# Moving the low parts of the attention output from VectorE to GpSimd, and reordering the first eight output-projection chunks

## The chip, the cores and the metric

One NeuronCore of a Trainium2 chip runs the whole program. The metric is the device time of one execution in microseconds (us). The engines are called PE (TensorE; its weight loads are shown as PEld), DVE (VectorE), ACT (ScalarE), POOL (GpSimd) and SP (SyncE, which only issues DMAs here).

## The reference, cut to what matters

The program computes two transformer-like blocks on 256 tokens of width 2048. The part around the change is the end of the first block's mixer, a gated delta rule with 32 value heads of 128 columns, and the output projection behind it:

```
def gated_deltanet(h, w_in, conv_w, a_log, dt_bias, norm_w, w_out):
    proj = h @ w_in
    ...
    o = gated_delta_rule(q, k, v, g, beta)            # [1, 256, 32, 128]
    o = o * lax.rsqrt(jnp.mean(o * o, -1, keepdims=True) + NORM_EPS)
    o = (o.astype(h.dtype) * norm_w) * jax.nn.silu(z.reshape(B, S, GDN_V_HEADS, HEAD_DIM))
    return o.reshape(B, S, GDN_DV) @ w_out            # [256, 4096] @ [4096, 2048]
x = layer_norm(ALPHA_DN * x + (1 + ga1) * y, ln_g[i, 0], ln_b[i, 0])
```

`ga1` is one sixth of `silu(c) @ mod_w + mod_b`, of which the kernel computes the last two thirds (`ga1` among them) beside the delta rule.

## The kernel before, in words

Every fp32 matrix product is made of three products of rounded operands: each operand is split into a high part (a copy to fp32r) and a low part (operand minus high part). For the weights ACT writes the high part `wh` (L1391, L1582) and another engine the low part `wl`: POOL at L597 while the delta rule runs, DVE at L2069 afterwards. One chunk of weights is 128x1024 numbers (two k-tiles by 512 columns, 512 KB), loaded by SP into a ring of four raw buffers; the split copies stand in a ring of three (`RING`) until the mixer is done, then of four. A chunk costs PE twelve matmuls.

The mixer works in 8 iterations (`NIT`) of four value heads. In each, PE interleaves the steps of `delta(it)` (some 20 small dependent pieces, which pass results between PE, DVE and ACT) with the 24 chunks of the next projection, by `beside`: one chunk, one step, except behind the chunks 3, 4 and 23 (`PAUSE`). In the last iteration there is no next input projection, and `ochunk(c)`, c = 0 to 23, does 24 chunks of the output projection instead (L830): chunks 0 to 11 for the output columns 0 to 511 (bank `pg[0]`), 12 to 23 for 512 to 1023 (`pg[1]`), each over heads 0 to 23. What is left, the last 8 heads of these two column groups (8 chunks, t = 0 to 7), and then all 32 heads of the other two groups (t = 8 to 39), is done by the loop `for t in range(CK_FF)` through `tchunk` (L1117). `out_chunk(t)` gives the bank, the pair of heads and whether it is the bank's last chunk.

The stationary operand of these chunks is the mixer's output `oT`, which is split too: `o_high(i)` on ACT (L1598) and `o_low(i)` on DVE (L2060) do four heads each, i = 0 to 7, as 128x1024 instructions. The group i = 7 is the output of the last iteration. In the last iteration DVE runs the steps of `delta`, an `o_low` behind each of the first five, and `mods` (L1818, L1820), which multiplies and sums the modulation weights that POOL loads (L591); the buffers of these loads are two, so POOL issues a load only when DVE is done with the one two before.

Around the end of the last iteration DVE does, in this order: `oz = ob * zt` (L2003), `low(0,0,0)`, the sum `md1`, `low(0,0,1)`, `oz * rstd` (L2014, counted as `on`), then `finish`, which copies PE's transposes of `oz` to `oT` with the norm weight (L2027), `low(0,0,2)` and `o_low(7)`. PE does the transposes (L726) behind chunk t = 0, and behind t = 2 it spreads `ga1` over the partitions (`row_of`, L1133, 32 matmuls). ACT copies `ga1` to SBUF (`ga1_out`, L1613) behind its copy for chunk 6, and DVE's `beside(t)` multiplies a finished bank by `ga1`, adds the residual and takes statistics (L2109, L2254, L2113), in order in its own queue between two `low`s: for `pg[0]` at t = 5, for `pg[1]` at t = 7.

Of the kernel before, what the change touches and what calls it, by code (L numbers as in the profile page):

```python
# [26 lines left out]
NIT = NQK // 2  # L27
# [56 lines left out]
def out_chunk(t):  # L84

    if t < 8:
        return t // 2 % 2, 12 + 2 * (t // 4) + t % 2, t in (5, 7)
    return 2 + (t - 8) // 16, (t - 8) % 16, (t - 8) % 16 == 15
# [28 lines left out]
def build(nc, A, out):  # L117
    ctx = ExitStack()
    with ctx:
# [276 lines left out]
        s_oh = sem("s_oh")  # L396
        s_os = sem("s_os")
        s_hm = sem("s_hm")
        s_ht = sem("s_ht")
# [67 lines left out]
        def _(sp):  # L467
# [77 lines left out]

            for half in range(2):
                for g in range(2):
                    loads(0, 0, 4 * half + 2 * g, w_out[:, 24 + 4 * half:28 + 4 * half, :], 512 * g, 2)
            for g in range(2):
# [34 lines left out]
        def _(pool):  # L584
# [40 lines left out]

            def batch(it, last=False):
                restart()
                rows = gcT[0:2 * NH, 0:P].unsqueeze(1).broadcast_to([2 * NH, VH, P])
                pick = pick2[:, bass.ds(it * VH, VH)].unsqueeze(2).broadcast_to([2 * NH, VH, P])
                nc.gpsimd.tensor_tensor(rowm[0:2 * NH], rows, pick, ALU.mult).then_inc(s_g, 1)  # L630
                for t in range(2):
                    mod_load(it * 8 + 32, t)
                for t in range(1, 22):
                    low(it + 1, t + 2)
                    if t >= 6 and t % 2 == 0 and t <= 16:
                        mod_load(it * 8 + 32, t // 2 - 1)
                if not last:
                    for t in range(RING):
                        low(it + 2, t)

            gcT = gx[:, 3, :]
# [7 lines left out]
            with pool.Fori(0, NIT - 1) as j:  # L649
                batch(j)  # L650
            batch(NIT - 1, True)

# [70 lines left out]
        def _(pe):  # L723
# [93 lines left out]
            def ochunk(c):  # L817

                if c == 0:
                    pe.wait_ge(s_zo, NIT)  # L820
                if c == 12:
                    pe.wait_ge(s_cd, NIT * 2)
                pe.wait_ge(s_low, NIT * NCH + (c + 5))
                g, kp = c // 12, c % 12
                if c < 12:
                    pe.wait_ge(s_os, kp // 2 + 1)
                for h in range(TT):
                    for k in range(2):
                        for i, (x, w) in enumerate(((0, wh), (0, wl), (1, wh))):
                            m = nc.tensor.matmul(halves(pg[g])[:, h, :], o_s[x][:, 2 * kp + k, h * P:(h + 1) * P],  # L830
                                                 w[c % RING][:, k, :], skip_group_check=True,
                                                 start=(kp == 0 and k == 0 and i == 0), stop=False)
                m.then_inc(s_pk, 1)
# [258 lines left out]
            for j in range(NIT - 1):  # L1092
                steps = beside(delta(j), steps, lambda c: gchunk(j + 1, c))
            steps = beside(delta(NIT - 1), steps, ochunk)

            def chunk(j, per, c, bank, act, k0, first, last):
# [48 lines left out]
            for t in range(CK_FF):  # L1145
                g, k, last = out_chunk(t)
                if t < 8:
                    pe.wait_ge(s_os, k // 2 + 1)
                elif t == 8:
                    pe.wait_ge(s_ev, 1)  # L1150
                elif t == 24:
                    pe.wait_ge(s_ev, 2)
                tchunk(0, 0, t, pg[g % 2], o_s, 2 * k, g >= 2 and k == 0, last)
                if t == 0:
                    next(steps)
                if t == 2:
                    pe.wait_ge(s_v, NIT * len(VO))
                    for i in range(2):
                        m = row_of(pd[i], 2 * KD + 8 * i)
                    m.then_inc(s_pp, 1)  # L1160
# [174 lines left out]
        def _(act):  # L1335
# [297 lines left out]
            def prep3():  # L1633
                act.wait_ge(s_pp, 5)
                for c in range(2):
                    a(BC[:, :, c, :], pd[c][:].rearrange("p (t s) -> p t s", s=P), ACT.Copy).then_inc(s_ap, 1)
            stream(0, 0, 0, CK_FF, {3: ga1_out, 15: prep0, 19: prep1, 24: prep2, 38: prep3})

# [135 lines left out]
        def _(dve):  # L1774
# [145 lines left out]
            def delta(it, mods):  # L1920
# [82 lines left out]
                done(v.tensor_tensor(oz, ob, zt, ALU.mult))  # L2003
                if not mods:
                    low(0, 0, 0)
                PEw("md1")
                mod_sum(it, 1)
                if mods:
                    squares(it + 1)
                else:  # L2010
                    low(0, 0, 1)
                dve.wait_ge(s_v, bv + VO["oz"])
# [41 lines left out]
            iteration(NIT - 2)  # L2054

            def o_low(i):

                dve.wait_ge(s_oh, i + 1)
                k = slice(4 * i, 4 * i + 4)
                v.tensor_tensor(fl(o_s[1][:, k, :]), fl(oT[:, k, :]), fl(o_s[0][:, k, :]).bitcast(F32),  # L2060
                                ALU.subtract).then_inc(s_os, 1)
            o_low(0)
            finish(NIT - 2)
            o_low(1)

# [19 lines left out]
            for t in range(18):  # L2085
                next(steps, None)
                if t < 5:
                    o_low(t + 2)
                mods(NIT * 8 + 24, t)
            finish(NIT - 1)  # L2090
            low(0, 0, 2)
            o_low(7)

# [392 lines left out]
```

## Time and profile before

| | |
|---|---|
| runs | 2819.94, 2822.1, 2823.57 us (median 2822.1) |
| profiled execution | 2822.1 us, span 2820.5 us, mean granted clock 0.987 |
| PE busy | 2710.6 us, 96% of the span |
| PEld, DVE, ACT, POOL busy | 83%, 69%, 43%, 28% |
| 868 to 970 us (last iteration), POOL busy | 60.20 us of 102.00 |
| 868 to 970 us, DVE busy | 79.32 us of 102.00 |

The span is the profile's own clock; 1.6 us of the execution lie around it. The rows below are from stretches of this span. The last iteration of the mixer fills it from about 865 to 967 us, and the eight chunks t = 0 to 7 from 964 to 991 us.

### The profile page before, as it was taken

The numbers are of one execution on the slowest core, as the hardware profiler recorded it, in microseconds if no ns is written. First come the engines' busy times: TensorE is split into PE (matmuls) and PEld (weight loads), VectorE is DVE, ScalarE is ACT, GpSimd is POOL, SyncE is SP. The second block draws the span as 40 slices with busy tenths as digits, with TensorE's granted clock in tenths as the row PEclk, the third lists the DMA queues.
The fourth block names the chain that finished last, engine by engine and source line by source line (L and its number), as shares of the span: only waits on it lengthen the run. The fifth ranks groups of instructions, "written<-read, shape, count | busy, mean of one in ns | idle before, by whom it ended". The sixth has DMA issues, their size and how long they took to land.

```text
span 2820.5 us, 48695 instructions
## 1 busy us (share of the span) xinstructions
PE 2710.6 (96%) x18902; PEld 2338.9 (83%) x18902; DVE 1949.8 (69%) x2291; ACT 1208.1 (43%) x1521; POOL 798.1 (28%) x548
## 2 busy tenths in 40 slices
PE   6999999999998999999999999969999999999998
PEld 4688988898897887888888888769999998888886
DVE  1377877787788677666666666676999899555554
ACT  2255455545545444333333333344333334543443
POOL 1056666676666510000000000001565562000000
PEclk8999999999999999999999999989999999999999
DMA  9866666666675666666666555535455554666664
GB/s 364 311 193 208 235 203 198 220 233 196 208 239 178 222 206 203 194 189 189 187 188 190 187 186 186 169 114 171 151 172 156 157 171 156 191 187 191 187 205 146
DMA packets 283912, 552.59 MB, mean 196 GB/s; under 512 B 16817, under 2 KB 54258, under 8 KB 282610
## 3 DMA queue, kind: packets, MB, share of 16 engines
q1 hardware_dynamic: 263632, 474.02, 53.4%
q0 software_dynamic: 19408, 76.06, 7.2%
q8 instruction: 122, 2.00, 0.3%
q10 hardware_dynamic: 722, 0.28, 0.0%
q14 instruction: 28, 0.23, 0.0%
HBM read 548.19 MB, written 2.10 MB: 195 GB/s over the span
## 4 chain that ended last, share of the span: by engine, by line
PE 82%; DVE 10%; ACT 4%; issue 2%; DMA 1%; DVEq 0%; POOL 0%; ACTq 0%; SPq 0%; POOLq 0%; PEld 0%
PE pg L1117 26%; PE pd L1117 17%; PE pg L811 13%; PE pg L1104 9%; PE pg L802 4%; PE pd L726 2%; DVE wl L2069 2%; PE pg L830 2%; DMA arena<-in_mod_w 1%; PE pd L991 1%; PE pd L973 1%; DVE arena L2348 1%; DVE arena L2350 1%; DVE arena L2343 1%; PE pd L739 1%
## 5 line engine op out<-in xcount | busy, mean ns | idle before, releaser
L2069 DVE TENSOR_TENSOR wl<-wr,wh 128x1024 fp32r<-128x1024 f32 x616 | 773.7, 1265 | 505.5 <-ACT wh L1582 502.2
L1582 ACT ACTIVATE wh<-wr 128x1024 fp32r<-128x1024 f32 x616 | 652.6, 1060 | 987.3 <-PE pg L1117 390.4
L597 POOL TENSOR_TENSOR wl<-wr,wh 128x1024 fp32r<-128x1024 f32 x195 | 479.3, 2459 | 404.1 <-ACT wh L1391 403.9
L1391 ACT ACTIVATE wh<-wr 128x1024 fp32r<-128x1024 f32 x216 | 227.7, 1057 | 346.5 <-PE pg L811 219.9
L1104 PE MATMUL pg<-hh,wh 128*128 128x256 f32 x1280 | 366.3, 286 | 3.8 <-ACT arena L1700 2.5
L1104 PE MATMUL pg<-hl,wh 128*128 128x256 f32 x1280 | 362.9, 284 | 0.0
L1104 PE MATMUL pg<-hh,wl 128*128 128x256 f32 x1280 | 362.7, 283 | 0.0
L1117 PE MATMUL pg<-wh,hh 128*128 128x512 f32 x832 | 327.2, 393 | 0.0
L1117 PE MATMUL pg<-wl,hh 128*128 128x512 f32 x832 | 326.3, 392 | 0.0
L1117 PE MATMUL pg<-wh,hl 128*128 128x512 f32 x832 | 325.4, 391 | 0.0
L811 PE MATMUL pg<-hh,wh 128*128 128x256 f32 x1024 | 300.8, 294 | 14.8 <-ACT arena L1439 12.0
L1820 DVE SCALAR_TENSOR_TENSOR arena<-arena,condt 128x512 f32<-128x512 f32 x240 | 281.6, 1174 | 24.1 <-DMA arena<-in_mod_w 18.6
L811 PE MATMUL pg<-hl,wh 128*128 128x256 f32 x1024 | 289.6, 283 | 0.0
L811 PE MATMUL pg<-hh,wl 128*128 128x256 f32 x1024 | 289.4, 283 | 0.0
L1104 PEld LDWEIGHTS pg<-hh,wh 128*128 128x128 f32 x1280 | 246.0, 192 | 16.0 <-issue 13.3
L715 POOL COPY arena<-arena 128x256 f32 x8 | 6.4, 797 | 875.5 <-ACT arena L1700 875.5
L1104 PEld LDWEIGHTS pg<-hh,wl 128*128 128x128 f32 x1280 | 246.1, 192 | 0.0
L1104 PEld LDWEIGHTS pg<-hl,wh 128*128 128x128 f32 x1280 | 246.0, 192 | 0.0
L811 PEld LDWEIGHTS pg<-hh,wh 128*128 128x128 f32 x1024 | 196.1, 191 | 33.4 <-ACT arena L1439 14.6
L811 PEld LDWEIGHTS pg<-hl,wh 128*128 128x128 f32 x1024 | 196.2, 192 | 0.2 <-issue 0.2
L811 PEld LDWEIGHTS pg<-hh,wl 128*128 128x128 f32 x1024 | 196.1, 191 | 0.0
L1117 PEld LDWEIGHTS pg<-wh,hh 128*128 128x128 f32 x832 | 156.4, 188 | 34.9 <-issue 0.4
(390 smaller groups left out, 5016.5 us busy)
## 6 DMA issues: line engine op xcount, KB each, us to landing
wr<-in_w_in SPq DMA_DIRECT2D x224, 512.0 KB, 3.9
wr<-in_ffn_w_gu SPq DMA_DIRECT2D x176, 512.0 KB, 4.2
wr<-in_gdn_w_in SPq DMA_DIRECT2D x128, 512.0 KB, 4.0
arena<-in_mod_w POOLq DMA_DIRECT2D x64, 1024.0 KB, 6.8
wr<-in_ffn_w_down SPq DMA_DIRECT2D x88, 512.0 KB, 3.8
arena<-in_mod_w SPq DMA_DIRECT2D x32, 1024.0 KB, 12.0
wr<-in_gdn_w_in SPq DMA_DIRECT2D x128, 256.0 KB, 2.9
wr<-in_gdn_w_out SPq DMA_DIRECT2D x56, 512.0 KB, 4.6
```

Of the source, the lines that this page charges most:

```text
L597: nc.gpsimd.tensor_tensor(wl[c % RING][:], wraw[c % 4], wh[c % RING][:].bitcast(F32), ALU.subtract)\
L726: return nc.tensor.transpose(dst, src, ident[0:n, 0:n])
L739: m = nc.tensor.matmul(pd[0][32 * i:32 * i + 32, 0:512], condt[:, k + i:k + i + 1].broadcast_to([P, 32]), wm[t % 6][:, i, :], start=(k == ...
L802: m = nc.tensor.matmul(halves(bank)[:, t, :], h_s[x][:, 2 * kp + k, t * P:(t + 1) * P], w[c % RING][:, k, :], skip_group_check=True, start ...
L811: m = nc.tensor.matmul(bank[:, n * T:(n + 1) * T], w[c % RING][:, k, n * P:(n + 1) * P], h_s[x][:, 2 * kp + k, :], skip_group_check=True, ...
L830: m = nc.tensor.matmul(halves(pg[g])[:, h, :], o_s[x][:, 2 * kp + k, h * P:(h + 1) * P], w[c % RING][:, k, :], skip_group_check=True, star ...
L1104: m = nc.tensor.matmul(bank[:, n * T:(n + 1) * T], w[s][:, k, n * P:(n + 1) * P], act[x][:, k0 + k, :], skip_group_check=True, start=(firs ...
L1117: m = nc.tensor.matmul(halves(bank)[:, h, :], act[x][:, k0 + k, h * P:(h + 1) * P], w[s][:, k, :], skip_group_check=True, start=(first and ...
L1391: a(wh[c % RING][:], wraw[c % 4], ACT.Copy).then_inc(s_hi, 1)
L1582: a(wh[c % 4][:], wraw[c % 4], ACT.Copy).then_inc(s_hc, 1)
L1820: m = stt(out=dst, in0=mw[t % 2][:, k, :], scalar=condt[:, kk:kk + 1], in1=dst, op0=ALU.mult, op1=ALU.add)
L2069: v.tensor_tensor(wl[c % 4][:], wraw[c % 4], wh[c % 4][:].bitcast(F32), ALU.subtract).then_inc(s_lc, 1)
```

## The change

Six of the eight `o_low` instructions (i = 1 to 6) go from DVE to POOL; the groups 0 and 7 stay on DVE and get a semaphore of their own, `s_osv`. The chunks t = 0 to 7 no longer alternate between the banks: four for `pg[0]`, then four for `pg[1]`. PE transposes the last heads ahead of chunk t = 0, `ga1` is spread behind t = 4, ACT copies it behind its copy for chunk 8, and DVE finishes `pg[0]` at t = 3. DVE's `low(0,0,0)` and `low(0,0,1)` go behind the last `delta` step.

```
-        return t // 2 % 2, 12 + 2 * (t // 4) + t % 2, t in (5, 7)
+        return t // 4, 12 + t % 4, t % 4 == 3
...
-            for half in range(2):
-                for g in range(2):
-                    loads(0, 0, 4 * half + 2 * g, w_out[:, 24 + 4 * half:28 + 4 * half, :], 512 * g, 2)
+            for g in range(2):
+                loads(0, 0, 4 * g, w_out[:, 24:32, :], 512 * g, 4)
...  POOL, last iteration
+                if o_low:
+                    o_low(1)
                 for t in range(2):
                     mod_load(it * 8 + 32, t)
                 for t in range(1, 22):
+                    if o_low and t < 6:
+                        o_low(t + 1)
                     low(it + 1, t + 2)
...
+            def o_low(i):
+                pool.wait_ge(s_oh, i + 1)
+                k = slice(4 * i, 4 * i + 4)
+                nc.gpsimd.tensor_tensor(flat4(o_s[1][:, k, :]), flat4(oT[:, k, :]), flat4(o_s[0][:, k, :]).bitcast(F32),
+                                        ALU.subtract).then_inc(s_os, 1)
...  PE
-                if c < 12:
-                    pe.wait_ge(s_os, kp // 2 + 1)
+                if c == 0:
+                    pe.wait_ge(s_osv, 1)
+                elif 2 <= c < 12:
+                    pe.wait_ge(s_os, kp // 2)
...
             steps = beside(delta(NIT - 1), steps, ochunk)
+            next(steps)
...
                 if t < 8:
-                    pe.wait_ge(s_os, k // 2 + 1)
+                    pe.wait_ge(s_os, 6)
+                    if k >= 14:
+                        pe.wait_ge(s_osv, 2)
...
-                if t == 0:
-                    next(steps)
-                if t == 2:
+                if t == 4:
                     pe.wait_ge(s_v, NIT * len(VO))
...  ACT
-            stream(0, 0, 0, CK_FF, {3: ga1_out, 15: prep0, 19: prep1, 24: prep2, 38: prep3})
+            stream(0, 0, 0, CK_FF, {5: ga1_out, 15: prep0, 19: prep1, 24: prep2, 38: prep3})
...  DVE, last iteration
             for t in range(18):
                 next(steps, None)
-                if t < 5:
-                    o_low(t + 2)
                 mods(NIT * 8 + 24, t)
+            low(0, 0, 0)
+            low(0, 0, 1)
             finish(NIT - 1)
```

POOL at the start of the last iteration, before. `rowm` is L630; `mod_w` rows are the modulation loads; the three `wl` buffers are the low parts of the chunks 3, 4, 5, 6, 7, 8 in turn.

```order
L630 TENSOR_TENSOR arena<-arena,masks 64x512
L591 DMA arena<-in_mod_w 128x4x512 x2
L597 TENSOR_TENSOR wl0_61<-wr,wh0_57 128x1024
L597 TENSOR_TENSOR wl1_62<-wr,wh1_58 128x1024
L597 TENSOR_TENSOR wl2_63<-wr,wh2_59 128x1024
```

The same place now; `ol` is the low part of `oT`.

```order
L630 TENSOR_TENSOR arena<-arena,masks 64x512
L650 TENSOR_TENSOR ol_52<-arena,oh_51 128x1024
L591 DMA arena<-in_mod_w 128x4x512 x2
L650 TENSOR_TENSOR ol_52<-arena,oh_51 128x1024
L597 TENSOR_TENSOR wl0_61<-wr,wh0_57 128x1024
L650 TENSOR_TENSOR ol_52<-arena,oh_51 128x1024
L597 TENSOR_TENSOR wl1_62<-wr,wh1_58 128x1024
L650 TENSOR_TENSOR ol_52<-arena,oh_51 128x1024
L597 TENSOR_TENSOR wl2_63<-wr,wh2_59 128x1024
```

One `ol` stands ahead of the two loads, and one ahead of each of the low parts of the chunks 3 to 7.

DVE at the end of the last iteration, before.

```order
L2003 TENSOR_TENSOR arena<-arena 128x1024
L2069 TENSOR_TENSOR wl0_61<-wr,wh0_57 128x1024
L2019 TENSOR_REDUCE arena<-pd0 128x4
L2022 TENSOR_TENSOR modt<-arena,vc 128x4
L2069 TENSOR_TENSOR wl1_62<-wr,wh1_58 128x1024
L2014 TENSOR_TENSOR arena<-arena 128x1024
L2027 TENSOR_SCALAR arena<-pd1,vc 128x2x4x128
```

The same place now (L2018 is the former L2003, L2025 the former L2014, L2038 the former L2027).

```order
L2018 TENSOR_TENSOR arena<-arena 128x1024
L2030 TENSOR_REDUCE arena<-pd0 128x4
L2033 TENSOR_TENSOR modt<-arena,vc 128x4
L2025 TENSOR_TENSOR arena<-arena 128x1024
L2074 TENSOR_TENSOR wl0_61<-wr,wh0_57 128x1024
L2074 TENSOR_TENSOR wl1_62<-wr,wh1_58 128x1024
L2038 TENSOR_SCALAR arena<-pd1,vc 128x2x4x128
```

The product for the transposes stands two `wl` instructions earlier.

DVE at the chunks t = 2 to 4 now: the low parts of the chunks 5 and 6, the small factors, the finishing of bank `pg0`, and the low part of chunk 7 (`wl3`) and of chunk 8.

```order
L2074 TENSOR_TENSOR wl1_62<-wr,wh1_58 128x1024
L2074 TENSOR_TENSOR wl2_63<-wr,wh2_59 128x1024
L447 ISA
L2105 TENSOR_SCALAR arena<-modt 128x16
L2106 TENSOR_TENSOR arena<-vc,arena 128x16
L2107 TENSOR_TENSOR arena<-vc,arena 128x16
L2108 TENSOR_TENSOR arena<-arena,modt 128x16
L447 ISA
L2116 TENSOR_TENSOR pg0<-pg0,arena 128x1024
L2261 SCALAR_TENSOR_TENSOR arena<-arena,pg0 128x2x512
L2120 BN_STATS arena<-arena 128x6 x2
L2074 TENSOR_TENSOR wl3_64<-wr,wh3_60 128x1024
```

Before, the low parts of the chunks 7 and 8 stood ahead of the finishing of `pg0`.

## Rows read from the trace of the kernel before

**Rows 1.** PE's timeline: start us, us, engine, line, operation, operands, [idle before, releaser].
```profile
880.76 0.39 PE L830 MATMUL pg<-wh,oh 128*128 128x512 f32 x1
...
892.65 1.15 PE L973 MATMUL pd<-arena 64*64 64x64 f32 x32 [1.87 <-DVE arena L1963]
893.73 0.50 PE L830 MATMUL pg<-wh,oh 128*128 128x512 f32 x1
...
898.69 1.83 PE L991 MATMUL pd<-arena 64*64 64x64 f32 x32 [1.95 <-DVE arena L1971]
```

**Rows 2.** Chain that ended last, 855 to 1010 us: start us, us, piece.
```profile
886.22 2.79 DVE arena L1820
...
900.52 3.82 PE pg L830 x12
...
905.41 2.94 PE pg L830 x12
```

**Rows 3.** Busy time in windows: length, PE, PEld, DVE, ACT, POOL, PEclk, DMA, GB/s.
```profile
899.00:902.00 3.00, 3.00 (x34) 2.59 (x31) 3.00 (x2) 0.00 (x0) 1.33 (x1) 0.50 0.50 128
...
970.00:983.00 13.00, 13.00 (x75) 11.09 (x74) 6.00 (x6) 5.27 (x7) 8.35 (x14) 1.00 0.91 312
```

**Rows 4.** POOL's timeline, last iteration and the one before it.
```profile
766.93 1.03 POOL L630 TENSOR_TENSOR arena<-arena,masks 64x512 f32<-64x512 f32 x1
...
867.07 2.02 POOL L630 TENSOR_TENSOR arena<-arena,masks 64x512 f32<-64x512 f32 x1
869.04 1.56 POOL L591 DMA_DIRECT2D arena<-in_mod_w  x2
...
882.61 8.63 POOL L597 TENSOR_TENSOR wl<-wr,wh 128x1024 fp32r<-128x1024 f32 x3 [0.99 <-ACT wh L1391]
...
894.18 2.40 POOL L597 TENSOR_TENSOR wl<-wr,wh 128x1024 fp32r<-128x1024 f32 x1 [1.32 <-ACT wh L1391]
```

**Rows 5.** DVE's timeline, last iteration.
```profile
884.23 1.98 DVE L2060 TENSOR_TENSOR ol<-arena,oh 128x1024 fp32r<-128x1024 f32 x1
...
894.16 3.75 DVE L1820 SCALAR_TENSOR_TENSOR arena<-arena,condt 128x512 f32<-128x512 f32 x2
...
904.63 1.53 DVE L1820 SCALAR_TENSOR_TENSOR arena<-arena,condt 128x512 f32<-128x512 f32 x2
```

**Rows 6.** Chain that ended last, the chunks t = 0 to 7.
```profile
963.85 3.01 PE pg L1117 x12
966.86 1.06 PE pd L726 x8
...
973.51 3.57 PE pd L1133 x32
977.08 32.92 PE pg L1117 x143
```

**Rows 7.** ACT's timeline, end of the iteration and `ga1_out`.
```profile
963.42 0.21 ACT L1527 ACTIVATE arena<-arena 128x8 f32<-128x8 f32 x1
...
982.78 1.02 ACT L1614 ACTIVATE arena<-pd 128x1024 f32<-128x1024 f32 x1
...
985.22 1.06 ACT L1582 ACTIVATE wh<-wr 128x1024 fp32r<-128x1024 f32 x1 [0.48 <-DMA wr<-in_gdn_w_out]
```

**Rows 8.** DVE's timeline, end of the iteration and the finishing of `pg[0]`.
```profile
965.56 1.22 DVE L2014 TENSOR_TENSOR arena<-arena 128x1024 f32<-128x1024 f32 x1
967.96 1.28 DVE L2027 TENSOR_SCALAR arena<-pd,vc 128x1024 f32<-128x1024 f32 x1 [1.19 <-PE pd L726]
969.16 1.22 DVE L2069 TENSOR_TENSOR wl<-wr,wh 128x1024 fp32r<-128x1024 f32 x1
...
987.46 1.23 DVE L2109 TENSOR_TENSOR pg<-pg,arena 128x1024 f32<-128x1024 f32 x1
988.72 1.22 DVE L2254 SCALAR_TENSOR_TENSOR arena<-arena,pg 128x1024 f32<-128x1024 f32 x1
989.98 1.43 DVE L2113 BATCH_NORM_STATS2 arena<-arena 128x6 f32<-128x512 f32 x2
```

More of the change, by code:

```diff
@@ L397, in build @@
         s_os = sem("s_os")
+        s_osv = sem("s_osv")
         s_hm = sem("s_hm")
@@ L624, in _, with batch @@
                                         pattern=[[2 * s, nb], [0, s]], channel_multiplier=-1).then_inc(s_cst, 1)
-            def batch(it, last=False):
+            def batch(it, o_low=None):
                 restart()
@@ L636, in batch @@
                         mod_load(it * 8 + 32, t // 2 - 1)
-                if not last:
+                if not o_low:
                     for t in range(RING):
                         low(it + 2, t)
+            def o_low(i):
+                pool.wait_ge(s_oh, i + 1)
+                k = slice(4 * i, 4 * i + 4)
+                flat4 = lambda x: x.rearrange("p a b -> p (a b)")
+                nc.gpsimd.tensor_tensor(flat4(o_s[1][:, k, :]), flat4(oT[:, k, :]), flat4(o_s[0][:, k, :]).bitcast(F32),
+                                        ALU.subtract).then_inc(s_os, 1)
             gcT = gx[:, 3, :]
@@ L650, in _ @@
                 batch(j)
-            batch(NIT - 1, True)
+            batch(NIT - 1, o_low)
             restart()
@@ L2003, in delta @@
                 done(v.tensor_tensor(oz, ob, zt, ALU.mult))
-                if not mods:
-                    low(0, 0, 0)
                 PEw("md1")
@@ L2009, in delta @@
                     squares(it + 1)
-                else:
-                    low(0, 0, 1)
                 dve.wait_ge(s_v, bv + VO["oz"])
@@ L2054, in _ @@
             iteration(NIT - 2)
[L2056 to L2062, printed above, removed]
+            dve.wait_ge(s_oh, 1)
+            v.tensor_tensor(fl(o_s[1][:, 0:4, :]), fl(oT[:, 0:4, :]), fl(o_s[0][:, 0:4, :]).bitcast(F32),
+                            ALU.subtract).then_inc(s_osv, 1)
             finish(NIT - 2)
-            o_low(1)
             def low(j, per, c):
@@ L2086, in _ @@
                 next(steps, None)
-                if t < 5:
-                    o_low(t + 2)
                 mods(NIT * 8 + 24, t)
+            low(0, 0, 0)
+            low(0, 0, 1)
             finish(NIT - 1)
             low(0, 0, 2)
-            o_low(7)
+            dve.wait_ge(s_oh, 8)
+            v.tensor_tensor(fl(o_s[1][:, 28:32, :]), fl(oT[:, 28:32, :]), fl(o_s[0][:, 28:32, :]).bitcast(F32),
+                            ALU.subtract).then_inc(s_osv, 1)
             def factors():
```

## The prediction

> **What bounds the kernel now.** I read the page first: PE is busy in 96% of the span, so a wait of PE that is added or removed moves the end, and nearly nothing else does. Then the chain of waits and PE's own timeline in the last iteration of the mixer, to see where PE waits there. Between 868 and 899 us it does. It waits 1.87 us and 1.95 us for DVE [rows 1], and where it starts again the granted clock is 0.50, so at its lower level of 1.2 GHz [rows 3]: a group of twelve matmuls takes 3.82 us instead of 2.94 [rows 2]. Behind 905 us the chain stays on PE until 1010 us, with no wait longer than an issue gap. The reader should see two regimes in one iteration: up to 899 us the small engines set the pace, and from 905 us PE does.
>
> The third view is the pair of timelines of POOL and DVE in the same stretch. DVE's two instructions of L1820 take 1.53 us together when POOL is idle (the one at 904.63) [rows 5], that is 0.77 each. In the chain at 886 us each takes 2.8 us [rows 2]. POOL then does three instructions in a row, 8.63 us from 882.61, so 2.88 each instead of 2.40 [rows 4]. At 894.18 POOL starts one of 2.40 us and DVE's pair beside it takes 3.75 us [rows 4, 5]: it ends at 897.91, which is POOL's end at 896.58 plus 1.33. So a DVE instruction with two operands in SBUF doesn't run beside a POOL instruction; it waits for its end, and POOL in turn waits about 0.5 us for it. The page "SBUF — State Buffer" of the Trainium skill, section "Who interferes with whom", says that such a pair shares a port as an exclusive lock and that the order of issue decides who waits; by that rule too, the trace agrees.
>
> **Part one: six `o_low` go to POOL.** On DVE one of them is 1.2 us alone and up to 2.9 beside POOL (1.98 in [rows 5]). On POOL it has the shape of `low`, so 2.40 us alone and 2.88 where DVE's instructions come between. POOL's queue is in order, and the new order puts one ahead of the low part of each of the chunks 3 to 7, which PE needs. The step count:
> - `rowm` (1.03 us uncontended [rows 4]) starts at 867.1 as before [rows 4] and ends about 868.1. It took 2.02 there because an `o_low` of DVE stood in its way, now gone. `o_low(1)` ends at 870.5, the two loads (1.56 us [rows 4]) at 872.1, 1.5 us later than before. DVE's product behind `rn` now finds POOL issuing loads and loses no time; it keeps POOL off until 872.8.
> - Two instructions per chunk: low(3) at 877.4 (PE asks for it a chunk ahead of 880.76, at 878.0: no wait), low(4) at 882.3 (2 x 2.40 plus a short DVE piece). PE asked at 880.76 [rows 1]: 1.5 late.
> - From here DVE always has something that wants the port, so a pair is 2 x 2.88 = 5.76 us: low(5) at 888.1, low(6) at 893.8, low(7) at 899.4. PE asked for chunk 7 at 893.73 [rows 1], so that chunk is 5.7 late.
> - What is given back: PE's old wait of 1.95 behind chunk 7 disappears behind the new one, and so may the half clock, which cost 3.82 - 2.94 = 0.9 on the group and some 1.2 on the 32 small matmuls ahead of it (1.83 us [rows 1], against about 0.6 for such a piece at full clock). With chunk 7 ending at 902.2 and DVE's next answer about 1.1 later, chunk 8 runs from 903.9 to 906.9. Before it ended at 904.3 (900.52 + 3.82 [rows 2]). That is 2.5 late.
> - What is then taken again: DVE's own queue. It has lost the `o_low`, but five L1820 and other two-operand pieces that met an idle POOL now each meet a busy one and wait up to 2.4 us. I put the reply for chunk 9 at 909.3, so it runs from 910.4 where it ran from 905.41 [rows 2]: 5.0 late. From chunk 10 on PE sets the pace again, without slack in which to catch up.
>
> By this walk the iteration ends 4.5 us late (between 4 and 5; I take off a half because my handover at each port change is rounded up). Bounds: if POOL and DVE did not disturb each other at all, ten POOL instructions of 2.40 from 872.1 end at 896.1, chunk 7 is 2.4 late, and the old wait and half clock behind it (1.95 + 2.1) come back: -1.7. If every handover goes against PE and DVE, +7. That the mod loads are issued 1.5 us later costs nothing beyond this; DVE asks for them about as late.
>
> The page "Perfetto Trace Analysis" of the Trainium skill, section "Optimizing Scalar/DVE Operations", warns that moving work between GpSimd and DVE might not help since they share a read port. By that rule alone the relief of DVE would be about nothing; it leaves open who is in the queue behind, which is where I put the loss.
>
> **Part two: the end of the iteration and the eight chunks.** Let C be the end of PE's last mixer chunk, 963.8 before. Before, chunk t = 0 starts at C [rows 6], and PE does eight chunks of 2.76 us (32.92 / 143 x 12 [rows 6]), the transposes (1.06) and `row_of` (3.57), 26.7 us without a wait.
> - Now the transposes come first. They need DVE's L2014, which needs `rstd`, done by ACT at 963.63 [rows 7], so C - 0.2. DVE's 1.22 [rows 8] gives C + 1.1, the transposes C + 2.2. Chunk t = 0 needs `low(0,0,0)`, which follows L2014, at C + 2.2 as well. Eight chunks and `row_of` are 25.65, so without further waits C + 27.9: 1.1 us lost. `o_low(7)`, needed at t = 2 now (C + 7.7), is done at C + 6.9: `finish` 1.2, `low` 1.2 and itself 1.2 behind C + 3.4 [rows 8]. No wait.
> - Chunk 7's low part now stands behind the finishing of `pg[0]` in DVE's queue, which waits for `ga1`. `row_of` ends at C + 2.2 + 5 x 2.76 + 3.57 = C + 19.6; ACT's two copies of about 1.0 [rows 7] end at C + 21.5; DVE's 1.23 + 1.22 + 1.43 [rows 8] at C + 25.4; low(7) at C + 26.6. PE asks for it at C + 2.2 + 7 x 2.76 + 3.57 = C + 25.1. A wait of 1.5.
> - ACT's copy for chunk 8 stands ahead of `ga1_out`, and it needs its DMA. Before, one of these copies waited for its DMA until 985.22, C + 21.4 [rows 7], with 312 GB/s and a DMA share of 0.91 from 970 to 983 us [rows 3]: the residual `x` and four weight chunks land together. Now two more weight chunks are asked for just ahead of this burst, because their buffers come free later. If chunk 8's DMA lands at C + 21.4 again, `ga1` is ready at C + 24.4, low(7) at C + 29.5, and PE waits 4.4.
>
> So part two costs 1.1 + 1.5 = 2.6 at least and 1.1 + 4.4 = 5.5 where DMA is late. I take 4, the middle, as the burst is shifted by some 2 us and widened by 1 MB. What the edit gives, an earlier finished `pg[0]`, is worth nothing: chunk t = 8, which needs it, ran without a wait before (the 143 matmuls of [rows 6] have no gap). Swapping the order of the weight loads moves the same bytes: nothing, between -0.3 and +0.3 by the 0.48 us wait in [rows 7].
>
> **Sum.** 4.5 + 4.0 = 8.5 us on the profiled execution's own 2822.1 (span 2820.5 and 1.6 around it), which is also the median of the runs: 2830.6 us. All that follows is paced by PE or by loads that follow PE, so the delay is carried to the end.
>
> **Rivals.**
> 1. *POOL keeps up, and DVE's relief is what counts* (faster). The chain from 872 to 899 us runs through DVE, and if chunk 7's low part were ready before 893.7 the waits 1.87 + 1.95 and the half clock, 2.1, would go: -5.9, less 2.6 of part two: -3.3, so 2818.8. Against it: ten POOL instructions do not fit in 872.1 to 893.7 even at 2.40. It decides at that one time. 6%.
> 2. *Both small* (no difference that shows). Port conflicts cost little, -1.7, part two 2.6 to 4: +0.9 to +2.3; or one of the two parts is half of what I say, up to +5: 2823 to 2827. 19%.
> 3. *The clock falls more often* (slower still). By the walk above PE now waits some 1.5, 3.0, 1.4, 1.7 and 2.4 us between 880 and 910 us. Before, two waits of 1.9 were followed by a stretch at the lower level that cost 2.1. Two such stretches on chunks where PE sets the pace add 2 x 2.1: 2834.8. For it: DVE and POOL hide only what falls into their waits. 17%.
> 4. *The forecast*, 2827 to 2833. 58%.
>
> **Range and chances.** The forecast's own range is 2826.5 to 2833. Taking in the case without port conflict with a prompt DMA (2823) and the sum of both upper ends, 7 + 5.5 with one more clock stretch of 2.1 (2836.7), I give 2823 to 2836.5. Two tenths of a percent, 5.6 us, is about what this measurement can tell from no change. Rival 1 gives 5% faster; rival 2 and the low edge of the forecast 21% within; the rest 74% slower.
>
> **What would show it.** In the new profile POOL's instructions stand back to back from 872 to 902 us, and PE waits for POOL's L597 line (its new number) ahead of the chunks 4 to 7: about 1.5, 3, 1.4 and 1.7 us. The time per group of twelve matmuls behind 915 us is unchanged. The transposes come 1.1 us behind the last mixer chunk. PE waits for DVE's low part ahead of t = 7, between 1.5 and 4.4 us, and the releaser of DVE's finishing of `pg[0]` is ACT's copy of `ga1`. I am wrong if POOL has gaps ahead of chunk 7's low part, if DVE's L1820 take 0.8 us each beside a busy POOL, or if chunk 8's DMA has landed before `row_of` ends, which would take 2 to 3 us off.

## The result, and the profile after

| | before | changed |
|---|---|---|
| median of the runs | 2822.84 us (2819.94 to 2824.7) | 2840.74 us (2836.88 to 2842.76, 4 runs) |
| ratio | | 1.0064, 95% interval 1.0051 to 1.0078 |
| profiled execution, span | 2822.1, 2820.5 us | 2838.75, 2836.8 us |
| mean granted clock | 0.987 | 0.984 |

The changed kernel is slower by 17.9 us. The forecast was 2830.6 us, 8.5 slower, with a range that ended at 2836.5: the sign was right, the size was not. Here is the same chain of waits as in [rows 2], of the changed kernel (start us, us, piece):

```profile
870.89 9.26 DVE arena L1948
880.19 3.69 PE pd L936 x16
...
904.79 4.76 DVE arena L1835
909.57 0.76 DVE arena L1835
910.36 0.70 DVE arena L1991
911.10 1.12 PE pd L738 x4
```

One DVE instruction of 9.26 us stands in it: L1948, the product behind `rn` (q and k times their inverse norms), 128x1024 with both operands in SBUF. Before, it took 2.47 us; alone such a shape takes 1.2 (1.23 in `port_guard` below). POOL's timeline beside it, the answer to [rows 4]:

```profile
868.15 1.56 POOL L591 DMA_DIRECT2D arena<-in_mod_w  x2
869.73 2.36 POOL L650 TENSOR_TENSOR ol<-arena,oh 128x1024 fp32r<-128x1024 f32 x1
872.05 2.39 POOL L597 TENSOR_TENSOR wl<-wr,wh 128x1024 fp32r<-128x1024 f32 x1
874.41 2.34 POOL L650 TENSOR_TENSOR ol<-arena,oh 128x1024 fp32r<-128x1024 f32 x1
876.72 2.33 POOL L597 TENSOR_TENSOR wl<-wr,wh 128x1024 fp32r<-128x1024 f32 x1
884.32 2.42 POOL L650 TENSOR_TENSOR ol<-arena,oh 128x1024 fp32r<-128x1024 f32 x1 [5.27 <-ACT oh L1613]
886.70 2.87 POOL L597 TENSOR_TENSOR wl<-wr,wh 128x1024 fp32r<-128x1024 f32 x1
```

Four instructions stand back to back from 869.73 to 879.05, and DVE's, which begins at 870.89, ends at 880.15, 1.1 us after POOL ran dry. Three times POOL passed from one instruction to the next and DVE was not let in between. From 884 us on the two do alternate, as the prediction had it: POOL's take 2.8 us instead of 2.4. Not everywhere, though: DVE's first L1835 in the chain above, 4.76 us from 904.79, is held in the same way, past one handover of POOL, until these two are over:

```profile
904.26 4.72 POOL L597 TENSOR_TENSOR wl<-wr,wh 128x1024 fp32r<-128x1024 f32 x2
```

The kernel before (product, and POOL's row beside it):

```profile
871.60 2.47 DVE L1933 TENSOR_TENSOR arena<-arena 128x1024 f32<-128x1024 f32 x1 [3.32 <-ACT arena L1467]
```

```profile
870.61 2.36 POOL L597 TENSOR_TENSOR wl<-wr,wh 128x1024 fp32r<-128x1024 f32 x1
873.54 2.77 POOL L597 TENSOR_TENSOR wl<-wr,wh 128x1024 fp32r<-128x1024 f32 x1 [0.57 <-ACT wh L1391]
```

There POOL happened to wait 0.57 us for ACT at 872.97, and the product ended 1.1 us after POOL fell idle. PE's waits in the changed kernel, the answer to [rows 1]:

```profile
880.19 3.68 PE L936 MATMUL pd<-arena 128*128 128x128 f32 x16 [5.21 <-DVE arena L1948]
...
895.20 0.50 PE L844 MATMUL pg<-wh,oh 128*128 128x512 f32 x1 [0.80 <-POOL wl L597]
...
900.77 0.50 PE L844 MATMUL pg<-wh,oh 128*128 128x512 f32 x1 [1.44 <-POOL wl L597]
...
904.84 1.15 PE L1005 MATMUL pd<-arena 64*64 64x64 f32 x32 [1.06 <-DVE arena L1986]
...
911.10 1.12 PE L738 MATMUL pd<-ident,arena 128*128 128x128 f32 x4 [2.14 <-DVE arena L1991]
...
973.42 1.09 PE L738 MATMUL pd<-ident,arena 128*128 128x128 f32 x8 [1.22 <-DVE arena L2025]
...
1002.23 0.77 PE L1132 MATMUL pg<-wh,oh 128*128 128x512 f32 x1 [4.55 <-DVE wl L2074]
```

The last two belong to part two. The chain into the last one, the answer to [rows 6] and [rows 7]; the mixer's last chunk ends at 972.2, which is C now:

```profile
981.48 12.40 DMA wr<-in_gdn_w_out
993.90 1.06 ACT wh L1597
994.96 0.05 ACT arena L1628
...
995.77 1.02 ACT arena L1629
...
996.88 1.24 DVE pg L2116
998.14 1.23 DVE arena L2261
999.40 0.70 DVE arena L2120
1000.13 0.70 DVE arena L2120
1000.86 1.24 DVE wl L2074
```

ACT's copy for chunk 8 (993.90) waits for its DMA ahead of the copy of `ga1`, DVE's finishing of `pg[0]` waits for that, and chunk 7's low part (1000.86) stands behind it. Behind three of these waits the granted clock is at its lower level, as in [rows 3]: it falls at 880.3, 911.0 and 999.7 us, where the kernel before has one such stretch, at 899 us. Two of the three (window: length, PE, PEld, DVE, ACT, POOL, PEclk, DMA, GB/s):

```profile
880.00:884.00 4.00, 3.81 (x19) 3.81 (x20) 3.38 (x12) 1.76 (x2) 0.00 (x0) 0.57 0.44 131
...
999.00:1007.00 8.00, 4.77 (x12) 3.83 (x13) 6.39 (x7) 0.00 (x0) 0.00 (x0) 0.57 0.42 133
```

What these stretches cost can be read from how far PE's starts shift against the other kernel, which does the same matmuls at full clock: 1.7, 1.5 and 1.9 us, against 1.3 us for the one of before. PE's waits of 0.45 us and more (without one of 0.91 for ACT at 871 us that both kernels have) add up to 10.65 us in the mixer, against 3.82 before, and to 5.77 in the tail, against none.

For all kernels one reading serves best: the start of matmul number k less that of number k before. All have 18,902 matmuls, so this shows where time is lost. In the profiled executions (us; the columns are times of the kernel before; "mixer" and "tail" are the differences between columns):

| kernel | at 845 | at 963 | at 1050 | mixer | tail | median less before's |
|---|---|---|---|---|---|---|
| changed | -2.2 | 8.4 | 16.2 | 10.6 | 7.8 | +17.9 |
| low_moved_only | -2.6 | 9.9 | 9.7 | 12.5 | -0.1 | +7.8 |
| tail_only | -0.5 | 1.1 | 7.2 | 1.6 | 6.1 | +4.6 |
| port_guard | -2.7 | 4.6 | 9.3 | 7.3 | 4.7 | +10.4 |
| ga1_before_copy8 | -2.4 | 10.7 | 15.5 | 13.1 | 4.8 | +13.5 |
| tail_row_of_early | -2.5 | -2.5 | -1.4 | 0.0 | 1.1 | +2.0 |
| loads_behind | -0.9 | 7.8 | 7.7 | 8.7 | -0.1 | +8.4 |
| spread | -2.9 | 12.7 | 12.6 | 15.7 | -0.1 | +14.2 |
| spread_guard | -2.3 | 9.7 | 9.6 | 12.0 | -0.1 | +10.9 |
| tiny_gap | -2.4 | 8.6 | 15.2 | 11.0 | 6.6 | +15.1 |
| o_low_later_on_dve | -2.5 | -0.4 | -0.5 | 2.1 | -0.1 | +1.3 |
| guard_row_of_early | -0.2 | 7.1 | 8.2 | 7.2 | 1.1 | +7.8 |
| half_on_pool | -2.5 | 3.3 | 4.4 | 5.9 | 1.1 | +4.3 |

Three cautions. Before 845 us no kernel differs from the one before, and all are 0.2 to 2.9 us ahead: that is what one execution differs from another by, and since all are ahead, it is mostly the profiled execution of before that is late. In the changed kernel's mixer 1.5 of the 10.6 us fall on a stretch at the lower clock level at 860 us, before anything the change touches delays PE; the change's part is 9.1. With the same POOL and DVE edits in the mixer, `low_moved_only` and `ga1_before_copy8` lose 12.5 and 13.1 there, so one execution gives part one only to some 4 us. And the differences of the medians, each against the runs of before on the same chip at the same time, are uncertain by 2.5 to 4 us by their intervals.

### The profile page after: what moved, and what is told of

Its sections match the earlier page's. It is cut to its first block, busy times and chain, and to the rows that moved or that the text cites. A ratio compares the mean times of both kernels' runs of the same rounds, so it can differ in the third digit from the quotient of the medians.

```text
span 2836.8 us, 48694 instructions
## 1 busy us (share of the span) xinstructions
PE 2715.5 (96%) x18902; PEld 2341.8 (83%) x18902; DVE 1948.6 (69%) x2285; ACT 1208.2 (43%) x1521; POOL 812.2 (29%) x554
## 4 chain that ended last, share of the span: by engine, by line
PE 80%; DVE 11%; ACT 4%; issue 2%; DMA 2%; DVEq 0%; POOL 0%; ACTq 0%; SPq 0%; POOLq 0%; PEld 0%
PE pg L1132 25%; PE pd L1132 17%; PE pg L823 13%; PE pg L1119 9%; PE pg L814 4%; DVE wl L2074 2%; PE pd L738 2%; PE pg L844 2%; DMA arena<-in_mod_w 1%; PE pd L987 1%; PE pd L1005 1%; DVE arena L2355 1%; DVE arena L2357 1%; DVE arena L2350 1%; ACT arena L1477 1%
## 5 line engine op out<-in xcount | busy, mean ns | idle before, releaser
L1597 ACT ACTIVATE wh<-wr 128x1024 fp32r<-128x1024 f32 x616 | 652.7, 1060 | 997.7 <-PE pg L1132 405.4
L1835 DVE SCALAR_TENSOR_TENSOR arena<-arena,condt 128x512 f32<-128x512 f32 x240 | 281.1, 1171 | 29.3 <-DMA arena<-in_mod_w 23.7
```

The costliest lines, as they stand in the source:

```text
L1597: a(wh[c % 4][:], wraw[c % 4], ACT.Copy).then_inc(s_hc, 1)
L1835: m = stt(out=dst, in0=mw[t % 2][:, k, :], scalar=condt[:, kk:kk + 1], in1=dst, op0=ALU.mult, op1=ALU.add)
```

## The experiments

The two parts apart. `low_moved_only` has the six `o_low` on POOL, with the chunks t = 0 to 7, the transposes, DVE's two `low`, `row_of` and `ga1_out` as before; `tail_only` is the rest of the diff, with the `o_low` on DVE.

> Part one alone: the six o_low on GpSimd, the eight chunks, the transposes, row_of, ga1_out and DVE's two low parts as before the change. Theory A (a DVE instruction with two SBUF operands is kept off the port by POOL instructions that follow each other without a gap, until POOL runs dry): DVE's product behind rn takes 8 to 10 us again instead of 1.2 or 2.5, PE waits about 5 us for it, and the kernel is 9 to 12 us slower than before. Rival B (only POOL's throughput, 2.4 to 2.9 us an instruction, as I forecast): 4 to 6 us slower, with the waits on POOL's low parts. Rival C (the two parts need each other): under 4 us.

> Part two alone: all o_low on DVE as before the change; new order of the eight chunks, transposes first, row_of behind t = 4, ga1_out behind the copy for chunk 8. If the parts add up: 1.1 us for the transposes and a wait of 1.5 to 4.5 us ahead of t = 7, and 2 to 3 us of half clock behind that wait, so 5 to 9 us slower than before. If the wait in the changed kernel came from part one's delay of the loads, it is under 2 us and the kernel is 1 to 3 us slower.

Measured: `low_moved_only` 2831.3 us (2830.48 to 2835.36), ratio 1.0036, interval 1.0022 to 1.0049; `tail_only` 2828.11, ratio 1.002, interval 1.0011 to 1.0029. Both parts cost. Neither median decides between its outcomes: 7.8 us slower lies below the 9 to 12 of theory A and above the 4 to 6 of rival B, and 4.6 below the 5 to 9 of parts that add up. The medians' 7.8 and 4.6 make 12.4, 5.5 less than the 17.9 of both together, which their intervals allow; in the traces the parts do add up, 12.5 and 6.1 against 10.6 and 7.8. So it is the trace that tells. Part one alone has the long product, longer still (10.77 us), and PE waits for it:

```profile
879.83 3.51 PE L937 MATMUL pd<-arena 128*128 128x128 f32 x16 [6.73 <-DVE arena L1950]
```

Here the product, by its start, is even first: POOL is still issuing its loads, and the row of instructions begins 0.38 us later. DVE, then POOL:

```profile
869.01 10.77 DVE L1950 TENSOR_TENSOR arena<-arena 128x1024 f32<-128x1024 f32 x1 [4.97 <-ACT arena L1484]
```

```profile
867.82 1.56 POOL L592 DMA_DIRECT2D arena<-in_mod_w  x2
869.39 2.39 POOL L651 TENSOR_TENSOR ol<-arena,oh 128x1024 fp32r<-128x1024 f32 x1
```

In `tiny_gap` and `spread` below it is the same, 0.37 and 0.41 us. Part two alone has the wait ahead of t = 7 behind the same chain, and a stretch at the lower clock level behind it (993.3 to 996.7 us):

```profile
993.79 0.77 PE L1118 MATMUL pg<-wh,oh 128*128 128x512 f32 x1 [3.46 <-DVE wl L2063]
```

Is it POOL's row that holds the product? `port_guard` is the changed kernel where POOL waits until the product is done before it starts `o_low(2)`. This adds a wait and takes no work away.

```
                 pool.wait_ge(s_oh, i + 1)
+                if i == 2:
+                    pool.wait_ge(s_v, (NIT - 1) * len(VO) + VO["qkn"])
```

> The changed kernel with one wait more: POOL waits for DVE's product behind rn before it does o_low(2). Theory A: DVE gets the port at once, the product takes 1.2 us instead of 9.3, PE's 5.2 us wait for it goes, what is left is POOL's throughput; 5 to 8 us faster than the changed kernel, so 10 to 13 us slower than before. Rival B (POOL's throughput alone): POOL starts its ten instructions about 0.7 us later and the kernel is 0 to 1 us slower than the changed one, 18 to 19 us slower than before.

Measured: 2833.92 us (2833.34 to 2835.55), ratio 1.0044, interval 1.003 to 1.0058, 6.8 below the changed kernel and as theory A had it. The product is back to the time that it takes alone, and POOL pays 1.0 for it; DVE's row and then POOL's:

```profile
868.94 1.23 DVE L1950 TENSOR_TENSOR arena<-arena 128x1024 f32<-128x1024 f32 x1 [4.96 <-ACT arena L1484]
```

```profile
870.32 2.41 POOL L652 TENSOR_TENSOR ol<-arena,oh 128x1024 fp32r<-128x1024 f32 x1 [1.01 <-DVE arena L1950]
```

So the cause of the product's 9 to 11 us is shown: POOL's row of instructions. Its price by the table is the mixer's 9.1 (product 9.3 us) or 12.5 (product 10.8) less 7.3, so 1.8 to 5.2 us; another 3.1 lie in the tail, 7.8 against 4.7, where the guarded execution had no stretch at the lower level and a wait of 3.5 instead of 4.5; that the guard is the cause of these is not shown. What then remains are the waits for POOL that the prediction had named:

```profile
880.43 0.50 PE L846 MATMUL pg<-wh,oh 128*128 128x512 f32 x1 [2.21 <-POOL wl L597]
...
885.54 0.50 PE L846 MATMUL pg<-wh,oh 128*128 128x512 f32 x1 [2.05 <-POOL wl L597]
...
896.70 0.50 PE L846 MATMUL pg<-wh,oh 128*128 128x512 f32 x1 [1.06 <-POOL wl L597]
```

and, behind them, 1.07 and 2.14 for DVE. The second of these stands behind the same L1835 (L1837 in this kernel) held by two POOL instructions, as in the changed kernel; the guard doesn't touch it.

The tail: `ga1_before_copy8` is the changed kernel with ACT's copy of `ga1` one place ahead (`{5: ga1_out` becomes `{4: ga1_out`), so that no DMA of chunk 8 stands in its way.

> The changed kernel with ACT's ga1_out one step earlier, ahead of its copy for chunk 8, so that it doesn't wait for that chunk's DMA. If the late DMA in ACT's queue is what makes the wait ahead of t = 7 4.5 us long: ga1 is copied right behind row_of, the wait falls to 1.5 to 2 us, and with it the half clock behind it; 3 to 5 us faster than the changed kernel, 13 to 15 slower than before. If DVE's finishing of the bank is late for another reason (the bank's last chunk, the residual), nothing changes: 17 to 19 us slower than before.

Measured: 2837.06 us (2836.19 to 2840.11), ratio 1.0054, interval 1.004 to 1.0068, which overlaps the changed kernel's. PE's wait ahead of t = 7 falls from 4.55 to 1.95, and ACT now waits for `row_of` itself, not for a DMA; PE and ACT:

```profile
1001.90 0.48 PE L1132 MATMUL pg<-wh,oh 128*128 128x512 f32 x1 [1.95 <-DVE wl L2074]
```

```profile
994.51 1.03 ACT L1628 ACTIVATE arena<-pd 128x1024 f32<-128x1024 f32 x1 [0.60 <-PE pd L1148]
```

The late DMA is therefore 2.6 us of the wait, the order of the queue the rest. The stretch at the lower clock level was expected to go with it; it is still there, but shorter (1002.7 to 1006.1 us). `tail_row_of_early` is `tail_only` with `row_of` back behind t = 2 and `ga1_out` behind the copy for chunk 6:

```
-                if t == 4:
+                if t == 2:
...
-            stream(0, 0, 0, CK_FF, {5: ga1_out, 15: prep0, 19: prep1, 24: prep2, 38: prep3})
+            stream(0, 0, 0, CK_FF, {3: ga1_out, 15: prep0, 19: prep1, 24: prep2, 38: prep3})
```

> Part two alone, but with row_of behind t = 2 and ga1_out behind the copy for chunk 6 as before the change; the new order of the chunks and the transposes ahead of t = 0 stay. If the late ga1 in DVE's queue is what part two costs beyond the transposes, the wait ahead of t = 7 and the half clock behind it go and 1.1 us is left: within 2 us of before, 3 to 4 us faster than part two alone. If the burst of loads (two more chunks beside the residual) costs by itself, PE still waits ahead of a chunk of 5 to 8, and it is 3 to 5 us slower than before.

Measured: 2824.39 us (2820.67 to 2828.15), ratio 1.0007, interval 0.9998 to 1.0016: no difference that can be told. The wait ahead of t = 7 is gone and the one of 1.22 ahead of the transposes is left, which is the tail's 1.1 in the table.

What decides whether DVE gets in? Three tries. `loads_behind` is `low_moved_only` with POOL's two modulation loads behind low(4), since the long case has DMA issues just ahead of the row and the alternating ones have none.

```
                 for t in range(2):
-                    mod_load(it * 8 + 32, t)
+                    if not o_low:
+                        mod_load(it * 8 + 32, t)
...
+                    if o_low and t == 2:
+                        mod_load(it * 8 + 32, 0)
+                        mod_load(it * 8 + 32, 1)
```

> Part one alone with POOL's two modulation loads behind the low part of chunk 4 instead of ahead of o_low(2). A look at the port, not at the time (the loads are some 7 us later, which costs several us by itself). If POOL keeps the port only in a row of instructions that begins behind its issue of DMAs, DVE's product behind rn now gets in at the first end of a POOL instruction and takes 2 to 3.5 us. If any row without a gap keeps DVE out, it takes 8 to 11 us as before.

Measured (one run): 2830.78 us, and the product unchanged, with five POOL instructions in a row and no DMA among them; DVE, then POOL:

```profile
870.70 9.25 DVE L1954 TENSOR_TENSOR arena<-arena 128x1024 f32<-128x1024 f32 x1 [4.97 <-ACT arena L1488]
```

```profile
867.17 4.73 POOL L655 TENSOR_TENSOR ol<-arena,oh 128x1024 fp32r<-128x1024 f32 x2
871.86 2.39 POOL L598 TENSOR_TENSOR wl<-wr,wh 128x1024 fp32r<-128x1024 f32 x1
```

That theory falls. `tiny_gap` puts an instruction that reads nothing between each of the first three `ol` in POOL's loop and the `wl` behind it:

```
                         o_low(t + 1)
+                    if o_low and t < 4:
+                        nc.gpsimd.memset(pad[:, t - 1:t], 0.0)
```

> The changed kernel with one short instruction more on POOL, a fill of one column, between each of the first three subtractions o_low(2), o_low(3), o_low(4) and the low part behind it; it writes an unused tile. Theory A, first form: DVE's product behind rn is kept off as long as POOL goes from one instruction with two SBUF operands straight into the next, and any instruction of POOL that reads no SBUF lets it in at its end. Then the product takes 2.0 to 5.5 us instead of 9.3 to 10.8, the gram matmuls wait under 2 us for it instead of 5.2, and the kernel is 3 to 7 us faster than the changed one: 2834 to 2838. Theory A, second form: DVE gets in only when POOL waits on a semaphore or has nothing to do; the product stays at 9 us or more and the time at 2840 to 2842. Theory B (the product is long for a reason of its own, not POOL's row): as the second form.

Measured: 2837.04 us (2836.76 to 2839.48), ratio 1.0056, interval 1.0041 to 1.0071. By its median alone the first form would stand (2834 to 2838), though its interval overlaps the changed kernel's; the product tells the forms apart, 10.85 us, and PE waits 6.81 for it. DVE, then POOL:

```profile
869.20 10.85 DVE L1951 TENSOR_TENSOR arena<-arena 128x1024 f32<-128x1024 f32 x1 [4.95 <-ACT arena L1485]
```

```profile
871.91 0.10 POOL L640 MEMSET pad<- 128x1 f32 x1
871.97 2.37 POOL L598 TENSOR_TENSOR wl<-wr,wh 128x1024 fp32r<-128x1024 f32 x1
874.30 2.33 POOL L653 TENSOR_TENSOR ol<-arena,oh 128x1024 fp32r<-128x1024 f32 x1
876.58 0.09 POOL L640 MEMSET pad<- 128x1 f32 x1
```

A short instruction is no gap; the second form stands. `spread` puts the `ol` wider apart in `low_moved_only` (ahead of the low parts of the chunks 4, 6, 8, 10, 12), and `spread_guard` adds the guard:

```
-                    if o_low and t < 6:
-                        o_low(t + 1)
+                    if o_low and t in (2, 4, 6, 8, 10):
+                        o_low(t // 2 + 1)
```

> Part one alone with its o_low(2) to (6) on POOL ahead of the low parts of the chunks 4, 6, 8, 10 and 12, where PE first needs them, instead of 3 to 7. Starvation theory: POOL still runs three instructions in a row over DVE's product behind rn (two instead of three missed ends), the product takes 6 to 9 us, and the kernel is 4 to 7 us slower than before. Throughput theory: POOL now has time, 1 us slower to 2 us faster than before.

> The same with POOL's wait for the product behind rn ahead of o_low(2). Both causes of part one's loss are then taken away: DVE's product takes 1.2 to 2.5 us, POOL's low parts come in time but for chunk 6 (about 1 us), and DVE has six instructions less. I expect 0 to 3 us faster than before. If the port conflicts of DVE's small pieces with a busier POOL are a cost of their own, it is 1 to 4 us slower.

Measured: `spread` 2836.57 us (2834.1 to 2837.57, without one execution of 7577), ratio 1.005, interval 1.0037 to 1.0063; `spread_guard` 2833.26 us (2832.16 to 2835.41), ratio 1.0039, interval 1.0026 to 1.0052. Both are misses. `spread` was to be 4 to 7 us slower than before and is 14.2; its product takes 8.51 us, as expected. I had expected `spread_guard` 0 to 3 us faster; it is 10.9 slower, though its product takes only 3.91 (one POOL instruction, the low part of chunk 3, stands ahead of the guard). The reason is the same mechanism at another place, in both kernels. L1839, which takes 0.75 alone, is held through three POOL instructions. In `spread_guard`, DVE, POOL, PE:

```profile
894.98 8.61 DVE L1839 SCALAR_TENSOR_TENSOR arena<-arena,condt 128x512 f32<-128x512 f32 x2
```

```profile
895.25 2.41 POOL L598 TENSOR_TENSOR wl<-wr,wh 128x1024 fp32r<-128x1024 f32 x1
897.61 2.35 POOL L653 TENSOR_TENSOR ol<-arena,oh 128x1024 fp32r<-128x1024 f32 x1
899.91 2.33 POOL L598 TENSOR_TENSOR wl<-wr,wh 128x1024 fp32r<-128x1024 f32 x1
```

```profile
904.37 1.98 PE L1008 MATMUL pd<-arena 64*64 64x64 f32 x32 [7.12 <-DVE arena L1990]
```

In `spread` the same pair (L1837 there) takes 10.58 us from 896.41, past three POOL instructions too, and PE waits 8.78 for what follows. One guard guards one instruction; any other may be the next.

Last, sizes and additivity. `guard_row_of_early` is the changed kernel with both mends, the guard and the early `row_of`. `half_on_pool` is that kernel with the pieces 3 and 5 back on DVE:

```
-                    if o_low and t < 6:
+                    if o_low and t in (1, 3, 5):
                         o_low(t + 1)
...  DVE
+                if t in (1, 3):
+                    dve.wait_ge(s_oh, t + 3)
+                    k = slice(4 * t + 8, 4 * t + 12)
+                    v.tensor_tensor(...).then_inc(s_osv, 1)
```

`o_low_later_on_dve` is the kernel before with three of its `o_low` one or two steps later in DVE's queue (`if t in (0, 1, 3, 4, 6): o_low((2, 3, 0, 4, 5, 0, 6)[t])`), a try for something faster than both.

> The changed kernel with both mends: POOL waits for DVE's product behind rn before o_low(2), and the tail's row_of stands at t = 2 with ga1_out one event ahead of the copies, as in the kernel before. If the two losses add up, this is 2840.7 - 6.8 (the guard's gain) - 3.7 (row_of's gain, measured with part two alone) = about 2830, that is 6 to 8 us slower than before. Rival: the losses overlap (the same weight transfer ends both waits), and this is within 1 us of the kernel with the guard alone, 2833 to 2835.

> The kernel with both mends, but pieces 3 and 5 go back to DVE, so POOL makes an o_low only for every second pair of output chunks (1, 2, 4, 6). The kernel with both mends is 7.8 us above the kernel before, and its trace shows TensorE waiting 5.3 us in three places for POOL's low parts wl. If what is left of part one is POOL's pace of one low part in 5.7 us while it makes an o_low between each two (the term that the prediction priced at 4.5 us), POOL now catches up after every second one: the waits for wl fall under 2 us in sum, and this is 2 to 5 us above before, 2824 to 2827. If what is left is DVE's own instructions being held longer while POOL works, it stays 6 to 8 us above before.

> The kernel before, with its three subtractions o_low(4), o_low(5), o_low(6) on DVE one to two steps of the last delta batch later, behind DVE instructions that the matmuls wait for; nothing goes to POOL and the tail is as before. If part of the kernel before is lost because these subtractions stand ahead of work that TensorE waits for, this is 0 to 2 us faster than before. If every one of them lies in slack already: within 1 us of before. If a later one makes an output chunk wait (its wait for os grows): 1 to 3 us slower, and the trace shows a wait of the ochunk matmuls for DVE o_low.

Measured: `guard_row_of_early` 2829.73 us (2829.09 to 2834.37), ratio 1.003, interval 1.0018 to 1.0042: +7.8, where losses that add were to give 6 to 8; its trace has the tail's 1.1 and the mixer's 7.2 side by side. `half_on_pool` 2826.29 us (2824.28 to 2830.4), ratio 1.0017, interval 1.0008 to 1.0026: +4.3, which fits POOL's pace (2 to 5 expected) but doesn't show it alone: the two intervals overlap, one wait of 2.38 for `wl` is left where under 2 was expected, PE also waits 1.47 and 2.51 for DVE, and the mixer still loses 5.9 us in the trace. `o_low_later_on_dve` 2823.23 us, ratio 1.0007, interval 0.9998 to 1.0016: the same as before. No kernel tried is faster than the one before.

## Why the prediction was wrong in size

**What bounds the kernel.** Right: the losses were waits of PE and the lower clock behind them, and behind 1050 us nothing was given back (the column stays within 0.1 us up to 2700 us: 16.22 and 16.27).

**Part one, the step that failed.** "DVE's product behind `rn` now finds POOL issuing loads and loses no time; it keeps POOL off until 872.8." It came at 870.89, when the loads were over (869.71) and `o_low(2)` ran. But its time isn't what decides: in `low_moved_only` it came at 869.01, while the loads were being issued, just as the prediction had it, and took 10.77 us. Even so the port rule of the prediction, each waits for the other's end, would have cost 1 or 2 us. The product lost 8, and PE waited 5.21 for it. What failed is thus the rule that a DVE instruction waits for the end of one POOL instruction, together with "loses no time". The Trainium skill's page "SBUF — State Buffer", section "Who interferes with whom", says that whoever issues first has the shared pair for the whole instruction, and that issue order decides who blocks. Read by the start times, it would have let DVE in at 872.05, since low(3) had not begun when DVE asked; here the trace doesn't agree, DVE was passed over at three ends, and in `low_moved_only` it started ahead of the whole row and was held all the same.

**Part one, the walk of POOL's queue.** Right in its order and nearly in its times, once the product is out of the way. In `port_guard`, which runs 2.7 us early, PE starts behind low(4), low(5) and low(7) at 880.4, 885.5 and 896.7, so 883.1, 888.2 and 899.4 on the clock of before; the walk said 882.3, 888.1 and 899.4. The waits were 2.2, 2.1, none and 1.1 for 1.5, 3, 1.4 and 1.7. (Two of its sums are 0.2 us off: 872.8 and two of 2.40 make 877.6, not 877.4, and 882.3 and three of 5.76 make 899.6, not 899.4.) The term of 4.5 measures 7.3 there, up to 1.0 of it the guard's own wait. The walk stopped at chunk 10, with "PE sets the pace again"; in the trace PE waits twice more for DVE, 0.57 at 911.87 and 0.70 at 916.25, and the loss grows by 1.0 (from 6.3 at 910 us to 7.3 at 940). In the changed kernel the same waits for POOL shrink to 0.8 and 1.44 since PE is late already. So part one is 9.1 in the changed kernel's execution, not 4.5 (alone, by the median, 7.8), and its upper bound of 7 was too low: "if every handover goes against PE and DVE" had been priced at one instruction for each handover.

**Part one, the given back.** The old wait of 1.87 did go. The one of 1.95 shrank to 1.06 at the same matmuls (L991 before, L1005 now), and one of 2.14 stands behind it that was not there, for DVE held by POOL once more. The old half clock went too, 1.3 us rather than 2.1, and two new ones came. The warning of the Trainium skill's page "Perfetto Trace Analysis", section "Optimizing Scalar/DVE Operations", that a move between GpSimd and DVE might not help, held: part one alone is +7.8 us.

**Part two.** Transposes 1.1 behind C: 1.22, right. The chain `row_of`, ACT, finishing, low(7): right in each link, and so was its late case. PE asked at 997.7, C + 25.5 (C + 25.1 forecast), and t = 7 began at C + 30.0 (C + 29.5). The step that failed is the choice: between 2.6 and 5.5 I took 4 as the middle, where [rows 7] had shown one of these copies waiting for its DMA until C + 21.4. In the changed kernel that copy started at 993.9, C + 21.7. The row was the better guide than the middle. Without the clock part two measures 1.2 + 4.55 = 5.8 in the changed kernel and 1.2 + 3.46 = 4.7 in `tail_only`, whose 6.1 in the table holds 1.4 of the lower clock.

**The clock (rival 3).** It priced two stretches more, 4.2 us. The changed kernel has three against one: in the mixer 1.7 + 1.5 less 1.3 = 1.9 us, which are within the 9.1, and in the tail, from 999.7 to 1006.5 us behind PE's wait of 4.55, 7.8 - 5.8 = 2.0 (1.9 by the shift of the starts). Rival 3 happened nearly whole, beside the forecast and not in its place; the forecast's own terms took half clock off and put none on.

**Sum.** 9.1 + 5.8 + 2.0 = 16.9 us, and 1.5 of a stretch at 860 us that the change has no part in; less the 2.2 by which this execution was ahead at 845 us, 16.2, against 16.65 between the profiled executions and 17.9 between the medians. Of the miss of 9.4 us, about half (4.6) is part one, 1.8 part two and 2.0 the clock of the tail; the last 1.0 is what the traces do not account for.

Left open: what decides which of the two manners, alternating or passed over, a DVE instruction meets. Not the DMA issues ahead of the row, not a short POOL instruction between, and not, by their start times, which of the two came first. The same instruction met the same manner in every kernel with the same row beside it.

## What to carry to other kernels

On this chip a queue of GpSimd instructions with SBUF operands, back to back, is not only a slower neighbour of VectorE: it can hold one two-operand VectorE instruction until the whole row is over (9.3 to 10.9 us for one of 1.2 here), and if TensorE waits for that instruction, the row's length is the price. Before filling GpSimd's gaps, find which VectorE instructions go through in them. In a queue that runs in order, what waits for a chain through three engines belongs behind the work that TensorE needs next; and where a row of the trace says when such a transfer lands, price that, not the middle of the cases.

## What was not expected of the hardware

A DVE instruction of 1.2 us took 9.3 to 10.9 us beside four POOL instructions of 2.3 to 2.4, and one of 0.75 took about 7.8 beside three (8.61 for the pair, of which the second is 0.75). In the long cases where POOL's row had not yet begun when DVE's instruction started, that did not help it (869.01 against 869.39, `low_moved_only`); beside such held instructions POOL's are at their shortest (2.33), where they take 2.8 when the two alternate. DVE instructions with one operand in PSUM were not held: the eight behind the product (L1953, in `port_guard` L1955) took 2.16 us in `port_guard` beside a busy POOL and 2.15 in the changed kernel when POOL was idle.
